# The gated rows of four feed-forward blocks turned by VectorE's block transposes and a trip through device memory, in place of TensorE's transposes

## The reference

```
x = x + 0.5 * swiglu_ffn(rms_norm(x, g), w13, w2)      # twice in the first block
h = h + swiglu(rms_norm(h, g), w_in, w_out)            # twice in the second

def swiglu_ffn(h, w13, w2):
    gate, up = split(h @ w13, 2)          # 1024 -> 2 x 2816
    return (silu(gate) * up) @ w2         # 2816 -> 1024
```

## Time and profile before

| | |
|---|---|
| three runs | 1265.01, 1265.20, 1266.54 us, median 1265.2 |
| the profiled execution | 1265.01 us, its span 1265.0 us |
| TensorE busy | 1252.4 us (99%) |
| VectorE busy | 759.2 us (60%) |
| ScalarE busy | 621.0 us (49%) |
| DMA | 212.27 MB, 51.2% of 16 engines' span |
| TensorE's mean granted clock | 0.997 |

### The profile page before, as it was taken

How to read it: one execution, slowest core, us unless ns; L and a number is a source line. 1 busy time by engine, 2 the same in 40 slices (tenths; PEclk the granted TensorE clock), 3 DMA queues, 4 the chain that set the end, 5 groups by cost and what they waited for, 6 DMA issues and landing times.

```text
span 1265.0 us, 16501 instructions
## 1 busy us (share of the span) xinstructions
PE 1252.4 (99%) x6711; PEld 1074.4 (85%) x6711; DVE 759.2 (60%) x891; ACT 621.0 (49%) x798; POOL 74.6 (6%) x127
## 2 busy tenths in 40 slices
PE   8999999999999999999999999999999999999998
PEld 6888888998888888899999888888888888888887
DVE  4654536897655545687677655554678546545445
ACT  5544336665544443655623544443466845444433
POOL 1000002002000000300001000000024000000000
PEclk9999999999999999999999999999999999999999
DMA  8866464452666564554202476645366417665530
GB/s 272 281 185 195 172 215 149 166 176 61 192 193 179 193 214 142 180 165 164 87 1 67 129 240 193 196 171 196 141 216 207 141 58 235 191 198 185 196 137 34
DMA packets 140427, 212.27 MB, mean 168 GB/s; under 512 B 10265, under 2 KB 101277, under 8 KB 140348
## 3 DMA queue, kind: packets, MB, share of 16 engines
q1 hardware_dynamic: 140352, 211.22, 51.2%
HBM read 210.14 MB, written 1.05 MB: 167 GB/s over the span
## 4 chain that ended last, share of the span: by engine, by line
PE 93%; DVE 3%; ACT 2%; POOL 1%; DMA 0%; issue 0%; SPq 0%; ACTq 0%; DVEq 0%; POOLq 0%
PE bank L1534 27%; PE bank L1536 27%; PE bank L1535 27%; PE bank L1944 2%; PE bank L1676 2%; PE bank L1955 1%; PE bank L1565 1%; DVE y L1132 1%; DVE wlo L1024 1%; PE bank L1917 1%; PE bank L1910 1%; PE bank L1871 1%; PE bank L1963 1%; DMA raw<-in_ffn_w_dram 0%; ACT whi L393 0%
## 5 line engine op out<-in xcount | busy, mean ns | idle before, releaser
L1024 DVE TENSOR_TENSOR wlo<-raw,whi 128x2048 fp32r<-128x2048 f32 (+1 forms) x190 | 416.6, 2196 | 286.2 <-ACT whi L393 286.2
L393 ACT ACTIVATE whi<-raw 128x2048 fp32r<-128x2048 f32 x190 | 362.9, 1914 | 233.8 <-PE bank L1536 224.9
L1534 PE MATMUL bank<-whi,xThi 128*128 128x512 f32 x1024 | 406.1, 397 | 2.5 <-DVE xTlo L1047 1.0
L1536 PE MATMUL bank<-whi,xTlo 128*128 128x512 f32 x1024 | 400.6, 391 | 0.0
L1535 PE MATMUL bank<-wlo,xThi 128*128 128x512 f32 x1024 | 400.1, 391 | 0.0
L1534 PEld LDWEIGHTS bank<-whi,xThi 128*128 128x128 f32 x1024 | 193.1, 189 | 42.7 <-issue 1.5
L1536 PEld LDWEIGHTS bank<-whi,xTlo 128*128 128x128 f32 x1024 | 193.0, 188 | 41.1
L1535 PEld LDWEIGHTS bank<-wlo,xThi 128*128 128x128 f32 x1024 | 193.3, 189 | 38.4
L1534 PE MATMUL bank<-whi,hThi 128*128 128x512 f32 x352 | 138.1, 392 | 0.0
L1536 PE MATMUL bank<-whi,hTlo 128*128 128x512 f32 x352 | 137.1, 390 | 0.0
L1535 PE MATMUL bank<-wlo,hThi 128*128 128x512 f32 x352 | 137.0, 389 | 0.0
(11 more groups left out here) (396 smaller groups left out, 1188.9 us busy)
## 6 DMA issues: line engine op xcount, KB each, us to landing
raw<-in_ffn_w_dram SPq DMA_DIRECT2D x176, 256.0 KB, 4.1
raw<-in_ffn_w_in_dram SPq DMA_DIRECT2D x176, 256.0 KB, 3.9
raw<-in_ffn_w_dram SPq DMA_DIRECT2D x22, 1024.0 KB, 4.9
raw<-in_ffn_w_out_dram SPq DMA_DIRECT2D x22, 1024.0 KB, 4.9
raw<-in_gdn_w_in_dram SPq DMA_DIRECT2D x16, 1024.0 KB, 5.3
raw<-in_w_in_dram SPq DMA_DIRECT2D x10, 1024.0 KB, 5.1
raw<-in_ple_w_gate_dram SPq DMA_DIRECT2D x8, 1024.0 KB, 4.9
raw<-in_w_kv_dram SPq DMA_DIRECT2D x8, 1024.0 KB, 5.9
```

Of the source, the lines that this page charges most:

```text
L393: act.activation(whi[w % SPLIT][:], raw[w % RAW][:], ACT.Copy).then_inc(w_hi, 1)
L1024: dve.tensor_tensor(wlo[w % SPLIT][:, c], raw[w % RAW][:, c], whi[w % SPLIT][:, c].bitcast(F32), ALU.subtract).then_inc(w_lo, 1)
L1534: pe.matmul(psum, lhs[0], rhs[0], start=start, stop=False, skip_group_check=True)
L1536: return pe.matmul(psum, lhs[1], rhs[0], start=False, stop=stop, skip_group_check=True)
```

## The change

TensorE's transposes of the gated rows are gone. In their place, for each hidden block:

1. VectorE transposes every 32x32 block of `hnat` by itself with one instruction, into `hblk`.
2. SP stores `hblk` (256 KB) to device memory (`hdram`, two buffers).
3. SP reads it back with four DMAs, one for each group of 32 partitions, in runs of 512 bytes, so that whole columns of 128 tokens come to stand on a partition (`hraw`).
4. ScalarE and VectorE make `hThi` and `hTlo` from `hraw` in place of a PSUM bank, one block later than before; those of the last two blocks are made within the down product.

Silu writes into `hnat`, and the product is made in place. `hThi` and `hTlo` have another order of tiles, which `tile` in TensorE's program follows. The store of block (f, j) stands in SP's program before the load of slot s + 10, the reads before that of slot s + 11, where s is the block's first slot.

```
+        hdram = [nc.dram_tensor(f"hidden{i}", [P, 4, P], F32, kind="Internal").ap() for i in range(2)]
...
+        rows_out = {up_slot(f, j) + 6: (f, j) for f in range(4) for j in range(NBLK)}
+        cols_in = {up_slot(f, j) + 7: (f, j) for f in range(4) for j in range(NBLK)}
...
@@ SP, ahead of the load of slot w
+                if w - RAW in rows_out:
+                    n = block_of(*rows_out[w - RAW])
+                    sp.wait_ge(sem("ffn_blk"), n + 1)
+                    if n >= 2:
+                        sp.wait_ge(*read(n - 2))
+                    sp.dma_start(hdram[n % 2], hblk[:, n % 2]).then_inc(wrote(n)[0], 16)
+                if w - RAW in cols_in:
+                    n = block_of(*cols_in[w - RAW])
+                    sp.wait_ge(*wrote(n))
+                    if n >= 2:
+                        sp.wait_ge(sem("ffn_lo"), n - 1)
+                    for i in range(4):
+                        sp.dma_start(hraw[32 * i:32 * i + 32, n % 2],
+                                     hdram[n % 2][:, i, :].rearrange("(b a) e -> a b e", a=32)).then_inc(read(n)[0], 16)
                 if w >= RAW:
                     sp.wait_ge(w_lo, split_done(w - RAW))
...
@@ ScalarE
                 def hidden_hi(j):
-                    act.wait_ge(sem("ffn_T"), NBLK * f + j + 1)
-                    act.activation(hThi[:, 2 * j:2 * j + 2, :], bank[4 + j % 2][:].rearrange("p (k c) -> p k c", k=2),
+                    n = block_of(f, j)
+                    act.wait_ge(*read(n))
+                    act.activation(hidden_tiles(hThi, j), hraw[:, n % 2].rearrange("p b (m q) -> p m b q", m=4),
                                    ACT.Copy).then_inc(sem("ffn_hi"), 1)
...
                     split(s + 2 + SPLIT)
-                    if j and not beside:
-                        hidden_hi(j - 1)
+                    if j >= 2 and not beside:
+                        hidden_hi(j - 2)
...
-                split(first[f"down{f}"] + SPLIT)
+                split(first[f"down{f}"] + SPLIT + 2)
+                hidden_hi(NBLK - 2)
+                split(first[f"down{f}"] + SPLIT + 4)
                 hidden_hi(NBLK - 1)
...
@@ VectorE (hidden_lo changed as hidden_hi is)
+                def hidden_blocks(j):
+                    n = block_of(f, j)
+                    dve.wait_ge(sem("ffn_h"), 2 * n + 2)
+                    if n >= 2:
+                        dve.wait_ge(*wrote(n - 2))
+                    dve.transpose(hblk[:, n % 2].rearrange("p i (m q) -> p m i q", m=4),
+                                  hnat[:, j % 2].rearrange("p t (k i q) -> p (t k) i q", k=2, i=4)).then_inc(sem("ffn_blk"), 1)
...
                     split(s + 2 + SPLIT)
-                    if j and not (f >= 2 and j == BESIDE):
-                        hidden_lo(j - 1)
+                    hidden_blocks(j)
+                    if j >= 2 and not (f >= 2 and j == BESIDE):
+                        hidden_lo(j - 2)
...
@@ TensorE
             def ffn(f):
-                def hidden_T(j):
...
-                    if j and not (f >= 2 and j == BESIDE):
-                        hidden_T(j - 1)
```

More of the change, by code:

```diff
@@ L184, in region @@
             return got
-        hThi, hTlo, hnat, silu, p_in, pThi, pTlo, pp, gate_s, row_chan, row_tap, row_tap4 = region(
-            [("hThi", [P, KF, SEQ], F32R), ("hTlo", [P, KF, SEQ], F32R),
-             ("hnat", [P, 2, NT, 256], F32), ("silu", [P, 2, NT, 256], F32)],
+        with ExitStack() as lent:
+            gate_s = lent.enter_context(nc.sbuf_tensor("gate_s", [P, NT, D], F32))
+        hThi, hTlo, hnat, hblk, hraw, p_in, pThi, pTlo, pp, row_chan, row_tap, row_tap4 = region(
+            [("hThi", [P, NBLK, 4, P], F32R), ("hTlo", [P, NBLK, 4, P], F32R),
+             ("hnat", [P, 2, NT, 256], F32), ("hblk", [P, 2, 4, P], F32), ("hraw", [P, 2, 4, P], F32)],
             [("p_in", [P, NT, PLE], F32), ("pThi", [P, 2, SEQ], F32R), ("pTlo", [P, 2, SEQ], F32R),
-             ("pp", [P, NT, D], F32), ("gate_s", [P, NT, D], F32)],
+             ("pp", [P, NT, D], F32)],
             [("row_chan", [CT, P], F32), ("row_tap", [TAPS, DC], F32), ("row_tap4", [W4, QKV * P], F32)])
+        hdram = [nc.dram_tensor(f"hidden{i}", [P, 4, P], F32, kind="Internal").ap() for i in range(2)]
         (gs, y, a_nat, ln_row, qz, kz, v1, mask1, mask_r, ident_r, diag, p2, pT1, yA, y_nat, flT, u, cumx, zf, zfe, lf,
@@ L294, in nth, with block_of, wrote, read @@
             return 2 * (n - (n > 8)) + t + 1
+        def block_of(f, j):
+            return NBLK * f + j
+        rows_out = {up_slot(f, j) + 6: (f, j) for f in range(4) for j in range(NBLK)}
+        cols_in = {up_slot(f, j) + 7: (f, j) for f in range(4) for j in range(NBLK)}
+        def wrote(n):
+            return sem(f"h_wrote{n % 2}"), 16 * (n // 2 + 1)
+        def read(n):
+            return sem(f"h_read{n % 2}"), 64 * (n // 2 + 1)
         def last_group(name):
@@ L406, in norm_sum @@
                     act.wait_ge(sem("norm_ss"), nth(FINAL + 1, t - 1))
-                spare = silu[:].rearrange("p a b c -> p (a b c)")
+                spare = hnat[:].rearrange("p a b c -> p (a b c)")
                 junk = spare if n in (FINAL, FINAL + 1) else xs[:, t, :]
@@ L1095, in ffn @@
                         dve.wait_ge(sem("ffn_silu"), 2 * (NBLK * f + j) + t + 1)
-                        if f or j >= 2:
-                            dve.wait_ge(sem("ffn_T"), NBLK * f + j - 1)
-                        dve.tensor_tensor(hnat[:, j % 2, t, :], silu[:, j % 2, t, :],
+                        dve.tensor_tensor(hnat[:, j % 2, t, :], hnat[:, j % 2, t, :],
                                           bank[2 * (j % 2) + t][:, 256:512], ALU.mult).then_inc(sem("ffn_h"), 1)
                     split(s + 2 + SPLIT)
-                    if j and not (f >= 2 and j == BESIDE):
-                        hidden_lo(j - 1)
+                    hidden_blocks(j)
+                    if j >= 2 and not (f >= 2 and j == BESIDE):
+                        hidden_lo(j - 2)
                     if f == 0 and j == 4:
                         setup()
-                split(first[f"down{f}"] + SPLIT)
+                split(first[f"down{f}"] + SPLIT + 2)
+                hidden_lo(NBLK - 2)
+                split(first[f"down{f}"] + SPLIT + 4)
                 hidden_lo(NBLK - 1)
@@ L1536, in passes, with tile @@
                 return pe.matmul(psum, lhs[1], rhs[0], start=False, stop=stop, skip_group_check=True)
+            def tile(x, k, t):
+                return x[:, k // 2, 2 * t + k % 2, :] if x is hThi or x is hTlo else x[:, k, t * P:(t + 1) * P]
             def ring(w):
@@ L1551, in rows @@
                     at = (k * len(psums) + c) * 512
[L1552 removed]
+                    ins = passes(psums[c][:], [tile(x, k0 + k, t) for x in src],
                                  [x[:, at:at + 512] for x in ring(w)], begins and k == 0, ends and k == nk - 1)
```

19 lines of the change are left out of this document (9 added, 10 removed).

## The result

| | before | after |
|---|---|---|
| median of four runs | 1265.23 us | 1244.89 us (1243.80 to 1245.64) |
| ratio, 95% interval | 1 | 0.9838 [0.9824, 0.9852] |
| span of the profiled execution | 1265.0 us | 1243.9 us |
| mean granted clock in it | 0.997 | 0.997 |
| DMA, share of 16 engines' span | 212.27 MB, 51.2% | 235.35 MB, 58.9% |

The change makes the kernel 20.3 us (1.6%) faster by the medians and 21.1 us by the two spans. Forecast were 1245.8 us and 19.4 us.

A forecast was written before the change was run, and what follows sets the result against it. TensorE's instruction issue in the feed-forward blocks was taken as the bound. From 1265.2 us, 19.4 went for the removed transposes (19.7 less 0.3), with 0 for added work and 0 for the clock: 1245.8 us, range 1242 to 1250.5.

The forecast's parts named there:

- The bound: Feed-forward blocks: the number of instructions TensorE issues sets the end, not who feeds it; TensorE busy 99%, 93% of the chain.
- The price of a group: TensorE, each hidden block: four transposes cost 0.447 us (0.36 plus 0.09 in a late successor); 44 groups, 19.7 us.
- The pricing by the listed duration: TensorE's 176 removed transposes charged in full at about 275 ns: 48 us, time 1217; the prediction rejected this.
- What was added: Per hidden block: VectorE's block transpose 0.68 us, ScalarE's copy 0.59, SP's store and four reads, DMA share near 0.8.
- The trip of block 5: First feed-forward block: block transpose done at 89.2, reads landed by 103.2, at worst 111.4; reckoned 14 us, at worst 22.
- The cost on the path: TensorE's path: the added transpose, store and reads cost 0, with 12.7 us of reserve before TensorE takes the weights.
- The profiled execution's time: Whole kernel before: profiled execution took 1265.01 us, its span 1265.0, so nothing lies around the span.
- The clock term: TensorE's two windows at 1.2 GHz: left at zero; both vanishing gives -3.2 us, three new ones +4.8.
- Rival 1: Turn of a hidden block: the 0.09 us penalty stays, only 44 x 0.36 = 15.8 us go; 1249.4 us, chance 0.04.
- Rival 2: Start, 34 to 46 us, DMA engines full: TensorE waits once, up to 8.4 us; 1254.2 us, chance 0.05.
- Rival 4: No gain: TensorE waits for another engine at the same places once it is faster; 1265 us, chance 0.03.
- Rival 3: ScalarE's wait for the reads: store to landing exceeds its room, slower; a 40 us trip gives 1323 us; chance 0.05.

## Why the prediction was right

- **The bound**: TensorE's own instructions in the feed-forward blocks. Right; the run with four idle transposes restores 1264.96 us.
- **The price of a group**: 0.447 us was too small. The pitches give 0.48. The error is in the interval that I took for an undisturbed product: from 84.71 to 95.18 I divided 10.47 us by 46 and got 0.2276, but the first of these intervals still stand under the group's effect. The trace of before shows it, in rows that I did not use:

```profile
87.47 0.39 PE L1536 MATMUL bank<-whi,xTlo 128*128 128x512 f32 x1
...
94.95 0.39 PE L1536 MATMUL bank<-whi,xTlo 128*128 128x512 f32 x1
```

The twelve intervals up to 87.47 took 0.230 each, the 33 from there to 94.95 0.2267, which is also 10.88 / 48 of the kernel after. 44 x 0.035 = 1.5 us is most of the difference between 19.4 and 21.1. The forecast time came closer to the median than this, 1245.8 against 1244.89, and that is luck: by the steps of their times, two of the four runs of after had two stretches at 1.2 GHz and one of the four of before, which puts the medians half a step apart and hid some 0.8 us of the gain.

- **The pricing by the listed duration**, with the Trainium skill's 275 ns (TensorE: Matmul & The Clock Gate, Part 4: PE-mode transpose): 48 us of gain. The runs say 0.11 us a transpose in a series, with 270 ns listed for each. The Trainium skill's figure, which it gives for bf16, is near the 270 listed here for float32; in a stream it is 2.5 times the cost.
- **What was added**: the block transpose took 0.70 us (0.68 taken), the copy from `hraw` 0.62 (0.59), the share of a block 0.82 (near 0.8), the rate 240 GB/s (240). The trip of block 5 ran from 87.44 (86.74 + 0.70) over SP's reads, issued from 94.68 to 96.65, to a landing the median 3.3 later, 12.5 us; forecast 14. The store was mis-sized: it took 5.1 us to land and not 2.0, so SP waited for it, and ScalarE waited for the reads twice where I had no wait. The cost on the path was 0 within what can be told, as the run without the trip shows.
- **The profiled execution's time**: I took 1265.01 us for it and wrote that nothing lies around its span. That was a misreading. For the kernel after, the profiled run took 1245.61 with a span of 1243.9, so 1.7 us lie outside; before it will have been the run of 1266.54. It moved nothing, since the same stands on both sides.
- **The clock term**: zero with bounds of -3.2 and +4.8. The two profiled executions had the same number of such stretches, so zero was right for them, but nothing in my working made it so; the medians mix runs a step of 1.6 us apart, and so 20.3 and 21.1 can both stand.
- **Rival 1** (the 0.09 belongs to the turn): out, products at the turn are 0.23 apart. **Rival 2** (start): no wait of TensorE there; ScalarE's waits for raw weights fell from 8.8 us to 7.6. **Rival 4**: out. **Rival 3** (the trip): it did not come about, and its room for one trip was near, 33.1 us against 34.4, but its mechanism was wrong twice. The delay reached TensorE through the PSUM bank, which came free within 0.5 us of the weights. And late trips in every block cost not from 34 us on but as soon as the loop over SP's program closes: with the reads one slot later, trips of 19 to 20 us, it is open; with two, 27 to 29, it is closed. The two gave 1242.52 and 1256.17.

## What to carry to other kernels

When one engine bounds a stretch, price what you take off it by the pitch of a repeated unit, with and without, and not by listed durations; one undisturbed interval must be read well away from the disturbance. Here a transfer of 12 us in every block, or of 19 to 20 in half of them, replaced work on the bound engine for nothing that can be told, since its result was asked for late enough. But check more than the distance from issue to use: follow every engine's fixed order round once, and see whether the next transfer's issue depends on this one's landing, since a loop longer than the pitch takes from the reserve in every round until it is gone.

## What the runs showed of the hardware

- fp32 128x128 transposes among products of 512 columns cost TensorE 0.11 us each and 0.04 us once a group, at a listed 270 ns (pitches of 10.88, 11.03, 11.36 and 11.79 us with none, one, four and eight in 48 products).
- Small ones cost less, but far from in proportion to their size: 24 transposes of 4 rows of 128 started within 1.55 us (46.16 to 47.71), 0.065 each, against 0.11 for 128 rows.
- VectorE's transposes of 32x32 blocks, 128x512 f32 in one instruction, took 0.704 us, hardly more than a subtraction of that size (0.68 in the earlier trace rows).
- Reads of 64 KB from device memory landed in 3.3 us in 512-byte runs and 3.4 in 128-byte runs; four times the runs raised a block's DMA share from 0.82 to 0.90.
- A wait of TensorE can cost more than itself: in the kernel with the reads two slots later waits of 3.1 and 5.4 us were each followed by a stretch at 1.2 GHz, with a granted clock of 0.66 and 0.67 in the 5 us behind. Such stretches also came where TensorE had not waited, as at 49.95 in the trace of before.
